# Time mix of a hybrid decoder step: the k and r projections as seven Strassen block products instead of eight

## The chip, the cores and the metric

One core of one Trainium2 chip runs the whole step. The metric is the device time of one execution in microseconds (us). TensorE does the matrix products, VectorE (DVE in the rows), ScalarE (ACT) and GpSimd (POOL) the elementwise work, and SyncE (SP) only starts transfers. All arithmetic is fp32.

## What is computed

The step has two branches fed by one input projection: latent attention (A) and an RWKV-7 time mix (B). This case is about B. Its input is `h` of 576 tokens (512 of a prompt and 8 samples of 8), 1024 channels; its projections r, k and v are 1024 x 1024 each:

```python
cols = jnp.einsum('btd,dn->btn', h, w_in)
...
xs = p + (prev - p) * mu_shift          # prev: the token before
r, wl, k, v, al = xs[..., :o1], xs[..., o1:o2], xs[..., o2:o3], xs[..., o3:o4], xs[..., o4:]
...
S = S * d_t - Sk[..., None] * (kk_t * a_t) + v_t[..., None] * k_t
```

A recurrence over the tokens follows (computed in chunks of 128 tokens, with the inverse of a triangular matrix per chunk and head), then a group norm, gates and the output projections.

## The kernel before

`rwkv` holds the time mix. Its main loop has eight passes, `i` = 0 to 7, one for each pair of heads (128 channels). Pass `i` does the recurrence of pair `i` and, between its dependent steps, the projections of pair `p = i + 1` (passes 0 to 6; the last pass fills the same places with gate projections, `gate_parts`). Each engine has its own queue, written out by hand in order, and waits on semaphores.

- The inverse has levels 0 to 5. At each, TensorE does `level_w`, ScalarE copies the result (`level` of the scalar part), TensorE does `level_x`, VectorE takes that up (`level` of the vector part: `copy_predicated` and a transpose), and the next level begins. TensorE fills the time between `level_w` and `level_x` with pieces of `project(p, q, steps)`: `q` = 0 is k, 1 is r, 2 is v. One step is one product of a 128 x 128 weight block with 288 tokens, and a projection is 16 steps: two halves of the tokens (`F0`, `F1`, 288 each) times eight blocks of channels. The profile counts two instructions for each fp32 step.
- A half's eight steps add up in one bank of PSUM. ScalarE then copies it to `px` and, scaled, to `xs` (`projected`); VectorE adds the token before it (`mix`). `keys`, `key_norms`, `key_max`, `roots` and `key_normed` normalise k. `decays` are three exponentials.
- At the start of a pass TensorE does the Gram matrices. VectorE takes the banks with `copy_predicated` (L2506, L2509) and starts the inverse with `begin_inverse`: four (or two) `copy_predicated` of 32 partitions (L2516) per group of units, whose mask `lev` and data `gram` are both in SBUF. TensorE's `token_major` (L1819) waits until VectorE has emptied the banks.
- GpSimd does little in this loop: `first_columns`, `last_columns` and `powers` (L1546, a power of 10 columns). Its queue is in that order: `powers(i - 1)` ends shortly after pass `i` began.
- `w` has four slots of weights; SP loads the next pair's into a slot (`next_w`) when the last product that reads it is done.

The stage behind the loop (`merge`) computes its own projections already by seven block products: `stationary_sums` and `moving_sums` there form operand sums on GpSimd (L2850 to L2866), `keep` copies partial sums on ScalarE, and `add` adds on VectorE (L3043 from PSUM and SBUF, L3045 from two SBUF tensors).

Of the kernel before, what the change touches and what calls it, by code (L numbers as in the profile page):

```python
# [13 lines left out]
P = 128  # L14
# [608 lines left out]
def prompt(nc, I, M):  # L623

    with ExitStack() as ctx:
# [32 lines left out]
        def _(sp):  # L658
# [769 lines left out]
EARLY_IN = 16 * (2 + 17 + 2)  # L1428
# [19 lines left out]
def rwkv(nc, I, O, M):  # L1448

    with ExitStack() as ctx:  # L1450
        sb = lambda name, shape: ctx.enter_context(nc.sbuf_tensor("rw_" + name, shape, F32))
        NU, C5, LAST = 2 * NB, NB, NP - 1
        gram, tm = sb("gram", [P, NU, 4, P]), sb("tm", [P, C5, 3, P])
# [7 lines left out]
        XT0, W5, Phi = sb("XT0", [RH, 2 * PB, RH]), sb("W5", [P, 2 * PB, RH]), sb("Phi", [P, PB, RH])  # L1461
        s_in, bkT, S = sb("s_in", [RH, BD, P]), sb("bkT", [P, 2, P]), sb("S", [P, PB + 1, P])
        bonus, M.ob = sb("bonus", [P, 2, USED]), sb("ob", [P, USED])
        o, om = sb("o", [P, NU, RH]), sb("om", [P, 2, NU])
        s_out, M.uvm = sb("s_out", [RH, BD, P]), sb("uvm", [P, BD, P])
        snT, oc, uv, sp_out, cen, gx, g = M.snT, M.oc, M.uv, M.sp_out, M.cen, M.gx, M.g
# [15 lines left out]
        lora_mm, sa_sb, proj, px_sb, pxs0, mixed, shc_sb = (sem(n) for n in ("lora_mm", "sa_sb", "proj", "px_sb", "pxs0", "mixed", "shc_sb"))  # L1482
        cum, expd, kkd, kf1_sb, kk_sum, kk_max, rooted, rk_prod, rk_sum, bonus_in, bonus_sb, prepared = (
# [14 lines left out]
        halves = (slice(0, RH), slice(RH, P))  # L1498
        F0, F1 = slice(0, HT), slice(HT, USED)
        ORDER, GATE_SLOT = (1, 0, 2), (1, 0, 2, 1)  # L1500
# [20 lines left out]
        def _(pool):  # L1521
# [25 lines left out]

            pool.wait_ge(tail.pv, G * (BD - 1))
# [32 lines left out]
        def _(sp):  # L1581
# [17 lines left out]
            def store_branch(p):  # L1599
                sp.wait_ge(ob_sb, p + 1)  # L1600
                sp.dma_start(M.ob_dram[:, p, 0:USED], M.ob[:, :]).then_inc(ob_stored, 16)
# [20 lines left out]
            def next_w(p, q):  # L1622
                sp.wait_ge(proj, 6 * p + 2 * q + 2)
# [38 lines left out]
            sp.wait_ge(M.cleared, 2)  # L1662
            store_branch(LAST - 1)
# [22 lines left out]
        def _(pe):  # L1686
# [43 lines left out]
            def project(p, q, steps):  # L1730
                for t in steps:
# [3 lines left out]
                    if k == 0:  # L1735
                        if q == 0:
                            if p:
                                pe.wait_ge(sa_sb, 4 * p + 3 + h)
                        elif q == 1:
                            pe.wait_ge(px_sb, 6 * p + h + 1)  # L1740
                        else:
                            pe.wait_ge(kk_max, p + 1)
                    last = mm(bank[h][:, 0:HT], w[:, ORDER[q], k, :], M.hT[:, k, (F0, F1)[h]], start=(k == 0), stop=(k == KT - 1))  # L1743
                    if k == KT - 1:
                        last.then_inc(proj, 1)

# [153 lines left out]
            def old_states(i):  # L1900
# [4 lines left out]
                for b in range(BD):  # L1905
                    last = tr(bank[2][:, b * RH:(b + 1) * RH], s_in[:, b, :], M.ident[0:RH, 0:RH])
# [79 lines left out]
            def out_to_tokens(i):  # L1986
                pe.wait_ge(oc_sb, i + 1)
                for c in range(PB):
                    last = tr(bank[6][:, c * P:(c + 1) * P], oc[:, c * P:(c + 1) * P], M.ident[:, :])
# [48 lines left out]
            for i in range(NP):  # L2038
# [39 lines left out]
                if more:  # L2078
                    project(p, 0, range(0, 5))
# [3 lines left out]
                if more:  # L2083
                    project(p, 0, range(5, 11))
# [5 lines left out]
                if more:  # L2090
                    project(p, 0, range(11, 16))
# [5 lines left out]
                if more:  # L2097
                    project(p, 1, range(0, 4))
# [5 lines left out]
                if more:  # L2104
                    project(p, 1, range(4, 8))
# [3 lines left out]
                if more:  # L2109
                    project(p, 1, range(8, 12))  # L2110
# [5 lines left out]
                if more:  # L2116
                    project(p, 1, range(12, 16))
# [5 lines left out]
                level_x(i, 5)  # L2123
                if more:
# [3 lines left out]
                prompt_y(i)  # L2128
# [40 lines left out]
        def _(act):  # L2169
# [21 lines left out]
            def projected(p, q, h):  # L2191
                n = ORDER[q]
                keep = M.omm[:, 8 * n + p:8 * n + p + 1]
                act.wait_ge(proj, 6 * p + 2 * q + h + 1)
# [1040 lines left out]
```

## Time and profile before

| | |
|---|---|
| median of 3 runs | 1559.08 us (1559.01 to 1562.05) |
| profiled execution, device time | 1559.9 us |
| its span, first to last instruction | 1558.3 us |
| mean granted TensorE clock | 0.992 of full speed |
| TensorE busy | 1509.3 us, 97% |
| VectorE, ScalarE, GpSimd busy | 823.8, 543.6, 223.6 us |
| main loop of the time mix | 686 to 1287 us, a pass of about 75 us |

The span is the time between the first and the last instruction; the device time is 1.6 us longer. Busy time of TensorE counts modelled ends of overlapping instructions, so starts of consecutive blocks are the better measure of what a block costs.

### The profile page before, as it was taken

Reading aid. Unit: us, or ns where it says so; the run is one execution under the profiler, and the core shown is the slowest. Engines: PE = TensorE matmul, PEld = TensorE weight load, DVE = VectorE, ACT = ScalarE, POOL = GpSimd, SP = SyncE. Lnnn points to the kernel's source line nnn. Section 1 sums busy time; section 2 is a strip of 40 time slices with the busy share of each in tenths; the row PEclk is TensorE's granted clock in tenths of the full one; section 3 lists DMA queues with packets and bytes.
Section 4 is the critical chain, followed back from the end, with each engine's and each line's share of the span. In section 5 each row is a group of like instructions: output and inputs, shape, how many; then the busy total and the mean of one; then the engine's idle time right before and its main releaser. Section 6 shows DMA issues by size and latency. Waiting matters only on the chain.

```text
span 1558.3 us, 36214 instructions
## 1 busy us (share of the span) xinstructions
PE 1509.3 (97%) x14666; PEld 1102.8 (71%) x14666; DVE 823.8 (53%) x1653; ACT 543.6 (35%) x1327; POOL 223.6 (14%) x279
## 2 busy tenths in 40 slices
PE   6999999999999999989999999999999999999998
PEld 4455576777888888767676767677777777777753
DVE  3154455557777777464656566656656522023422
ACT  3056445441222222336353535353535222210000
POOL 0000141220112120110000000000000045355200
PEclk9999999989999999999999999999999999999999
DMA  9713688832566663411111111111111116342302
GB/s 328 288 54 108 182 227 281 221 96 72 138 161 164 159 161 101 115 42 38 30 51 31 50 32 50 32 50 40 41 51 34 46 35 193 92 147 75 115 14 74
DMA packets 190674, 164.35 MB, mean 105 GB/s; under 512 B 38458, under 2 KB 169530, under 8 KB 189484
## 3 DMA queue, kind: packets, MB, share of 16 engines
q1 hardware_dynamic: 181228, 126.47, 29.0%
q0 software_dynamic: 8352, 32.52, 6.9%
q10 hardware_dynamic: 928, 3.05, 0.6%
q8 instruction: 116, 1.90, 0.5%
q14 instruction: 50, 0.41, 0.1%
HBM read 136.44 MB, written 25.56 MB: 104 GB/s over the span
## 4 chain that ended last, share of the span: by engine, by line
PE 83%; DVE 6%; ACT 5%; DVEq 2%; DMA 2%; issue 1%; SPq 0%; POOL 0%; ACTq 0%
PE me_bank L2929 12%; PE rw_bank L1743 10%; PE sa_psOs L1197 7%; PE sa_psS L1152 7%; PE me_bank L2949 4%; PE pr_psZ L738 3%; PE fr_bankL L307 2%; PE rw_bank L1782 2%; PE fr_bankL L247 2%; PE pr_psS L726 2%; PE sa_psT L1162 2%; DVE rw_gram L2506 2%; PE rw_bank L1844 2%; PE pr_psO L757 1%; PE rw_bank L1863 1%
## 5 line engine op out<-in xcount | busy, mean ns | idle before, releaser
L1743 PE MATMUL rw_bank<-hT,big 128*128 128x288 f32 x672 | 182.8, 417 | 0.0
L1743 PEld LDWEIGHTS rw_bank<-hT,big 128*128 128x128 f32 x672 | 121.9, 189 | 32.1 <-issue 1.2
L1254 ACT COPY kpe<-sa_psS 128x512 f32<-128x512 f32 x64 | 34.4, 589 | 137.3 <-PE sa_psS L1152 137.3
L738 PE MATMUL pr_psZ<-hT,qlT 128*128 128x288 f32 x256 | 74.1, 410 | 0.6 <-DVE pr_zraw L838 0.6
L1768 PE MATMUL rw_bank<-hT,big 128*128 128x288 f32 x256 | 73.5, 421 | 0.0
L1541 POOL COPY shc<-prep 128x3 f32<-128x3 f32 x8 | 1.5, 188 | 471.1 <-ACT rw_xs L2208 471.1
L2988 ACT COPY big<-me_bank 128x288 f32<-128x288 f32 x42 | 16.7, 398 | 144.8 <-PE me_bank L2929 144.8
L738 PEld LDWEIGHTS pr_psZ<-hT,qlT 128*128 128x128 f32 x256 | 47.5, 192 | 21.7 <-issue 10.1
L2526 DVE COPY_PREDICATED rw_X<-lev,rw_bank 128x128 f32<-128x128 int32 (+1 forms) x80 | 20.9, 261 | 77.5 <-PE rw_bank L1863 77.5
L1197 PE MATMUL sa_psOs<-big,sa_ST 128*128 128x257 f32 x256 | 60.3, 386 | 0.0
L1197 PE MATMUL sa_psOs<-pages,sa_ST 128*128 128x257 f32 x256 | 60.3, 385 | 0.0
L997 POOL DMA_DIRECT2D big<-in_cache_kv x68 | 37.6, 552 | 156.1 <-issue 156.1
L1768 PEld LDWEIGHTS rw_bank<-hT,big 128*128 128x128 f32 x256 | 44.9, 189 | 20.1 <-issue 11.5
L1343 DVE TENSOR_TENSOR sa_ST<-sa_psT,kinvp 128x512 f32<-128x512 f32 x64 | 42.9, 679 | 28.7 <-PE sa_psT L1162 28.6
L1197 PEld LDWEIGHTS sa_psOs<-pages,sa_ST 128*128 128x128 f32 x256 | 47.1, 189 | 11.0 <-issue 4.4
L1197 PEld LDWEIGHTS sa_psOs<-big,sa_ST 128*128 128x128 f32 x256 | 47.0, 190 | 11.3 <-issue 5.0
L997 POOL DMA_DIRECT2D pages<-in_cache_kv x68 | 37.5, 552 | 117.8 <-issue 117.2
L2929 PE MATMUL me_bank<-prep,me_arena 128*128 128x288 f32 x208 | 53.4, 406 | 0.0
L882 ACT COPY pr_pT<-pr_psT 128x128 f32<-128x128 f32 (+3 forms) x64 | 27.2, 425 | 59.9 <-PE pr_psT L747 59.9
L2929 PEld LDWEIGHTS me_bank<-prep,me_arena 128*128 128x128 f32 x208 | 39.5, 190 | 10.9
L1264 ACT ACTIVATE sa_ST<-sa_ST 128x1024 f32<-128x1024 f32 x32 | 33.8, 1057 | 37.5 <-DVE sa_ST L1366 36.8
L726 PE MATMUL pr_psS<-pr_kh,pr_qh 96*128 96x128 f32 (+3 forms) x128 | 45.8, 440 | 0.1
(564 smaller groups left out, 3373.2 us busy)
## 6 DMA issues: line engine op xcount, KB each, us to landing
big<-in_w_in SPq DMA_DIRECT2D x44, 512.0 KB, 4.0
big<-in_cache_kv POOLq DMA_DIRECT2D x68, 128.0 KB, 3.7
pages<-in_cache_kv POOLq DMA_DIRECT2D x68, 128.0 KB, 3.2
fr_wada<-in_w_ada SPq DMA_DIRECT2D x8, 1024.0 KB, 11.7
big<-in_cache_kv SPq DMA_DIRECT2D x60, 128.0 KB, 2.9
pages<-in_cache_kv SPq DMA_DIRECT2D x60, 128.0 KB, 3.1
qk_scratch<-oaT SPq DMA_DIRECT2D x32, 192.0 KB, 2.6
fr_wada<-in_w_ada SPq DMA_DIRECT2D x2, 2048.0 KB, 11.0
```

The costliest lines, as they stand in the source:

```text
L726: nc.tensor.matmul(psS[u % 3][:, 0:cols(u)], qh[hp % 2][:, hh, qb * P:(qb + 1) * P], kh[hp % 2][:, hh, 0:cols(u)], start=True, stop=True). ...
L738: last = nc.tensor.matmul(psZ[h][:, 0:HT], M.wz[hp % 2][:, k, :], M.hT[:, k, h * HT:(h + 1) * HT], start=(k == 0), stop=(k == KT - 1))
L997: e.dma_start(M.pages[s % 2][q * QP:(q + 1) * QP, g, :, 0:KL], src).then_inc(landed, 16)
L1152: done = nc.tensor.matmul(psS[:, b, 0:2 * P], q4[n % 2][rows, a, :], cT(i)[rows, a, :], start=False, stop=(a == NCB - 1))
L1197: done = nc.tensor.matmul(psO[:, 0:C1], STs[s % 2][:, GP * g + c, :], M.pages[s % 2][:, g, c, :], start=(g == 0 and c == 0), stop=False)
L1254: nc.scalar.copy(S.rearrange("q (c p j) -> q p c j", c=2 * GP, p=GP)[:, :, cs, :], got[:, :, cs, :]).then_inc(copied, 1)
L1264: nc.scalar.activation(part, part, ACT.Exp, scale=SCALE).then_inc(exped, 1)
L1343: v.tensor_tensor(group, psT[g % 2][:, :].rearrange("p (a h t) -> p a h t", h=H, t=TD), bc(ki, TD, 3), ALU.mult).then_inc(weighted, 1)
L1743: last = mm(bank[h][:, 0:HT], w[:, ORDER[q], k, :], M.hT[:, k, (F0, F1)[h]], start=(k == 0), stop=(k == KT - 1))
L1768: last = mm(bank[h][:, 0:HT], w[:, 3, k, :], M.hT[:, k, (F0, F1)[h]], start=(k == 0), stop=(k == KT - 1))
L2929: last = nc.tensor.matmul(into[:, 0:HT], st[:, k, :], mv[:, k, :], start=(k == 0 and n in (1, 2, 7)), stop=(k == KT // 2 - 1), skip_group_ ...
L2949: last = nc.tensor.matmul(out_bank[o][:, :], mT[k][:, b * P:(b + 1) * P], wo[k][:, n * 512:(n + 1) * 512], start=(k == 0), stop=(k == KT - 1))
```

## The change

k and r of pair `p` become one product of a 2 x 2 block matrix (k and r by low and high half of the 1024 channels) with a 2 x 2 block matrix (low and high channels by `F0` and `F1`). Strassen's form in Winograd's variant needs seven block products of four steps each, 28 steps in place of 32, for each of the seven pairs of the loop. The products are run in the order 1, 2, 6, 5, 3, 7, 4 into two banks. v stays as it was, and so do the projections of pair 0.

- GpSimd forms the sums of the moving operand once, in pass 0 (`moving_sums`: 16 operations of 288 columns), and those of the weights for each pair (`stationary_sums`: 4 of 128 columns, one of 512, and, after products 1 and 2 are done, 4 of 128 and one of 512 that overwrite weights in place).
- ScalarE copies the running sum of bank 0 to `px` after products 1, 6 and 5 (`keep_partial`), and scales from SBUF (`scaled_from_sbuf`).
- VectorE adds bank 1 to what was kept (`add_partial`), three times a pair.
- `key_norms` moves behind `prompt_y` on TensorE, `keys` behind `level(i, 5)` on ScalarE, `mix(p, 0)` behind `level(i, 4)` on VectorE.
- Room for the sums comes from sharing: `gate` is saved to DRAM early and loaded back in the last pass, `ob` shares with `bonus`, `oc` with `RT`, `XT0` with `W5`, `snT` with the spare columns of `hT`.

```diff
+            sp.wait_ge(M.front_done, 1)
+            sp.dma_start(M.gate_dram, M.gate[:, :]).then_inc(M.early_in, 16)
...
+            def moving_sums():
+                pool.wait_ge(prepared, 1)
+                pool.wait_ge(M.early_in, EARLY_IN)
+                for k in range(K4):
+                    q.tensor_tensor(T3[k], M.hT[:, K4 + k, F1], M.hT[:, k, F1], ALU.subtract)
+                pool.drain()
+                pool.wait_ge(M.oa_stored, 32)
+                for k in range(K4):
+                    q.tensor_tensor(T2[k], T3[k], M.hT[:, k, F0], ALU.add)
+                pool.drain()
+                for k in range(K4):
+                    q.tensor_tensor(T4[k], M.hT[:, K4 + k, F0], T2[k], ALU.subtract)
+                for k in range(K4):
+                    last = q.tensor_tensor(T1[k], M.hT[:, k, F1], M.hT[:, k, F0], ALU.subtract)
+                last.then_inc(summed, 1)
+
+            def stationary_sums(p):
+                a1, a2 = w[:, 1, :, :], w[:, 0, :, :]
+                pool.wait_ge(w_in[1], 16 * p + 16)
+                pool.wait_ge(w_in[0], 16 * p + 16)
+                for k in range(K4):
+                    q.tensor_tensor(S1[k], a2[:, k, :], a2[:, K4 + k, :], ALU.add)
+                pool.drain()
+                q.tensor_tensor(a2[:, 0:K4, :], a1[:, 0:K4, :], a2[:, 0:K4, :], ALU.subtract)
+                pool.drain()
+                pool.wait_ge(proj, proj_of(p, 1))
+                for k in range(K4):
+                    last = q.tensor_tensor(a1[:, k, :], S1[k], a1[:, k, :], ALU.subtract)
+                last.then_inc(summed, 1)
+                pool.drain()
+                pool.wait_ge(proj, proj_of(p, 2))
+                q.tensor_tensor(a1[:, K4:KT, :], a1[:, K4:KT, :], a1[:, 0:K4, :], ALU.subtract).then_inc(summed, 1)
...
             for i in range(NP):
+                if i == 0:
+                    moving_sums()
                 if i < LAST:
                     first_columns(i + 1)
+                    stationary_sums(i + 1)
                     last_columns(i + 1)
...
+            sp.dma_start(M.gate[:, :], M.gate_dram).then_inc(M.fixed_in, 16)
...
+            def multiply(p, n):
+                a1, a2 = w[:, 1, :, :], w[:, 0, :, :]
+                low, high = slice(0, K4), slice(K4, KT)
+                if n == 1:
+                    pe.wait_ge(w_in[1], 16 * p + 16)
+                    pe.wait_ge(sa_sb, 4 * p + 3)
+                elif n == 2:
+                    pe.wait_ge(sa_sb, 4 * p + 4)
+                elif n == 6:
+                    pe.wait_ge(kept, kept_of(p, 1))
+                    pe.wait_ge(summed, summed_of(p, 2))
+                elif n == 5:
+                    pe.wait_ge(kept, kept_of(p, 6))
+                elif n == 3:
+                    pe.wait_ge(kept, kept_of(p, 5))
+                    pe.wait_ge(summed, summed_of(p, 4))
+                elif n == 7:
+                    pe.wait_ge(added, added_of(p, 11))
+                elif n == 4:
+                    pe.wait_ge(w_in[0], 16 * p + 16)
+                    pe.wait_ge(added, added_of(p, 22))
...
                 level_w(i, 1)
                 if more:
-                    project(p, 0, range(0, 5))
+                    multiply(p, 1)
...
                 level_x(i, 1)
                 if more:
-                    project(p, 0, range(5, 11))
+                    multiply(p, 2)
...
                 level_w(i, 2)
                 if more:
-                    project(p, 0, range(11, 16))
+                    multiply(p, 6)
...
                 level_w(i, 3)
                 if more:
-                    project(p, 1, range(0, 4))
+                    multiply(p, 5)
...
                 level_x(i, 3)
                 if more:
-                    project(p, 1, range(4, 8))
+                    multiply(p, 3)
...
                 level_w(i, 4)
                 if more:
-                    project(p, 1, range(8, 12))
+                    multiply(p, 7)
...
                 level_x(i, 4)
                 if more:
-                    project(p, 1, range(12, 16))
+                    multiply(p, 4)
...
                 level_x(i, 5)
+                prompt_y(i)
                 if more:
                     key_norms(p)
                 else:
                     gate_parts(range(46, 47))
-                prompt_y(i)
...
                 level(i, 3)
-                if not more:
+                if more:
+                    keep_partial(p, 5)
+                    scaled_from_sbuf(p, 1, 0)
+                else:
                     gate_sigmoid(2)
                 blocks_in_place(i, 2)
                 if more:
                     decays(p)
+                    second_keys(p)
...
                 level(i, 4)
                 if more:
-                    projected(p, 1, 0)
+                    scaled_from_sbuf(p, 0, 1)
...
+                level(i, 5)
                 if more:
                     keys(p)
-                level(i, 5)
-                if more:
-                    projected(p, 1, 1)
+                    scaled_from_sbuf(p, 0, 0)
```

## Rows read from the trace of the kernel before

**Rows 1.** The page, part 1.

```profile
PE 1509.3 (97%) x14666; PEld 1102.8 (71%) x14666; DVE 823.8 (53%) x1653; ACT 543.6 (35%) x1327; POOL 223.6 (14%) x279
```

**Rows 2.** Windows: us, busy PE, PEld, DVE, ACT, POOL, then PEclk.

```profile
835.00:910.00 75.00, 72.87 (x1076) 54.61 (x1076) 45.76 (x102) 34.48 (x90) 2.47 (x4) 1.00 0.16 42
```

**Rows 3.** Waits of TensorE, 700 to 1260: total, times, longest.

```profile
PE rw_bank L1819 <- DVE rw_gram L2509: 5.3, 7, 1.1
PE rw_bank L1953 <- ACT rw_Y L2283: 2.0, 7, 0.3
```

**Rows 4.** Timeline of TensorE, 922 to 992: start, duration, line.

```profile
928.21 2.69 PE L1743 MATMUL rw_bank<-hT,big 128*128 128x288 f32 x10
930.83 0.88 PE L1863 MATMUL rw_bank<-rw_X,rw_W 32*32 32x32 f32 x72
931.64 3.18 PE L1743 MATMUL rw_bank<-hT,big 128*128 128x288 f32 x12
934.65 0.71 PE L1883 MATMUL rw_bank<-ident_sb,rw_o 128*128 128x128 f32 x5
...
942.26 2.21 PE L1743 MATMUL rw_bank<-hT,big 128*128 128x288 f32 x8
944.40 1.08 PE L1891 MATMUL rw_bank<-rw_uvm,rw_bkT 128*64 128x512 f32 x4
...
957.17 1.14 PE L1870 MATMUL rw_bank<-rw_XF,rw_W 64*64 64x64 f32 x16
```

**Rows 5.** Timeline of ScalarE, 922 to 992.

```profile
943.15 1.28 ACT L2186 ACT_TABLE_LOAD   x1
...
946.18 0.20 ACT L2189 ACTIVATE g<-gx 128x12 f32<-128x12 f32 x1
948.71 0.26 ACT L2244 COPY rw_W<-rw_bank 32x128 f32<-32x128 f32 x1 [2.34 <-PE rw_bank L1847]
...
954.20 1.06 ACT L2267 COPY rw_s_out<-rw_bank 64x512 f32<-64x512 f32 x2
...
956.75 0.64 ACT L2247 COPY rw_W<-rw_bank 64x256 f32<-64x256 f32 x2
957.41 0.35 ACT L2206 COPY prep<-rw_bank 128x224 f32<-128x224 f32 x1
...
958.15 1.17 ACT L2273 COPY rw_s0p<-rw_bank 64x512 f32<-64x512 f32 x2
```

**Rows 6.** Timeline of all engines, 763.9 to 765.5.

```profile
763.93 0.22 POOL L1537 COPY prep<-ssT 128x24 f32<-128x24 f32 x1
...
764.42 1.22 DVE L2516 COPY_PREDICATED rw_X<-lev,rw_gram 32x128 f32<-32x128 int32 x4
```

**Rows 7.** Lines by form, GpSimd, 880 to 1560.

```profile
L2861 POOL TENSOR_TENSOR me_arena<-big 128x512 f32<-128x512 f32 x10 | 12.9, 1292 | 50.6 <-DMA big<-in_w_pb 20.9 <-DMA big<-in_w_pa 16.1 <-DMA big<-in_w_in 13.6
...
L2850 POOL TENSOR_TENSOR prep<-hT 128x1152 f32<-128x1152 f32 x1 | 2.6, 2627 | 48.4 <-ACT rw_Y L2278 48.4
```

**Rows 8.** Line L3043 on VectorE: ns min, median, max.

```profile
L3043 DVE TENSOR_TENSOR big<-me_bank,big x24: 457/458/458, 1382.7 to 1496.5; 128x288 f32<-128x288 f32 x24
```

**Rows 9.** Line L3045 on VectorE, the same columns.

```profile
L3045 DVE TENSOR_TENSOR prep<-prep,big x8: 458/1110/2703, 1383.3 to 1455.0; 128x288 f32<-128x288 f32 x8
```

**Rows 10.** Timeline of all engines, 1400.1 to 1403.3.

```profile
1400.47 2.64 POOL L2851 TENSOR_TENSOR prep<-me_arena 128x1152 f32<-128x1152 f32 x1
1400.72 2.70 DVE L3045 TENSOR_TENSOR prep<-prep,big 128x288 f32<-128x288 f32 x1
```

**Rows 11.** Line L2516 on VectorE, columns as in rows 8.

```profile
L2516 DVE COPY_PREDICATED rw_X<-lev,rw_gram x80: 219/294/307, 691.6 to 1224.1; 32x128 f32<-32x128 int32 x64, 32x64 f32<-32x64 int32 x16
```

**Rows 12.** Timeline of VectorE, 691 to 699.

```profile
691.63 1.22 DVE L2516 COPY_PREDICATED rw_X<-lev,rw_gram 32x128 f32<-32x128 int32 x4
...
695.76 1.22 DVE L2516 COPY_PREDICATED rw_X<-lev,rw_gram 32x128 f32<-32x128 int32 x4
```

**Rows 13.** Windows of pass 0, columns as in rows 2.

```profile
691.00:694.00 3.00, 0.53 (x7) 0.16 (x3) 2.79 (x8) 0.00 (x0) 0.00 (x0) 1.00 0.01 1
694.00:697.40 3.40, 3.40 (x19) 2.74 (x20) 3.19 (x9) 0.98 (x4) 0.00 (x0) 0.52 0.00 0
```

More of the change, by code:

```diff
@@ L1425 @@
 HT = USED // 2
-EARLY_IN = 16 * (2 + 17 + 2)
+EARLY_IN = 16 * (1 + 2 + 17 + 2)
 def _load_vectors(sp, I, M):
@@ L1745, in project @@
                         last.then_inc(proj, 1)
+            def multiply(p, n):
[19 more added lines that the diff above has]
+                    pe.wait_ge(added, added_of(p, 22))
+                into = bank[1 if n in (2, 7, 4) else 0][:, 0:HT]
+                st = {1: a1[:, low, :], 2: a1[:, high, :], 3: a1[:, high, :], 4: a2[:, high, :], 6: a1[:, low, :], 7: a2[:, low, :]}
+                for k in range(K4):
+                    held = S1[k] if n == 5 else st[n][:, k, :]
+                    moving = {1: M.hT[:, k, F0], 2: M.hT[:, K4 + k, F0], 3: M.hT[:, K4 + k, F1], 4: T4[k], 5: T1[k], 6: T2[k], 7: T3[k]}[n]
+                    last = mm(into, held, moving, start=(k == 0 and n in (1, 2, 7)), stop=(k == K4 - 1), skip_group_check=True)
+                last.then_inc(proj, 1)
             def first_projections(q, h):
@@ L1905, in old_states @@
                 for b in range(BD):
-                    last = tr(bank[2][:, b * RH:(b + 1) * RH], s_in[:, b, :], M.ident[0:RH, 0:RH])
+                    last = tr(bank[2][:, b * RH:(b + 1) * RH], s_in[:, b, :], M.ident[halves[1], halves[1]])
                 last.then_inc(s_tr, 1)
@@ L1988, in out_to_tokens @@
                 for c in range(PB):
-                    last = tr(bank[6][:, c * P:(c + 1) * P], oc[:, c * P:(c + 1) * P], M.ident[:, :])
+                    last = tr(bank[6][:, c * P:(c + 1) * P], oc_of(i)[:, c * P:(c + 1) * P], M.ident[:, :])
                 last.then_inc(oc_tr, 1)
@@ L2301, in out_channels @@
                     act.wait_ge(M.oa_stored, 32)
-                a.copy(oc[:, :], bank[6][:, :]).then_inc(oc_sb, 1)
+                a.copy(oc_of(i), bank[6][:, :]).then_inc(oc_sb, 1)
             def last_state(i):
@@ L2465, in mix, with add_partial @@
                 stt(by_b(xs[:, n, SEQ:USED]), pxs[:, n, :, 0:TD], mu, by_b(xs[:, n, SEQ:USED]), ALU.mult, ALU.add).then_inc(mixed, 1)
+            def add_partial(p, n):
+                dve.wait_ge(proj, proj_of(p, {11: 2, 22: 7, 21: 4}[n]))
+                dve.wait_ge(kept, kept_of(p, {11: 1, 22: 5, 21: 6}[n]))
+                got = bank[1][:, 0:HT]
+                if n == 22:
+                    mine, own = px[:, 0, HT + 1:SEQ + 1], pxs[:, 0, :, 1:TD + 1]
+                    tt(mine, got[:, 0:SEQ - HT], mine, ALU.add)
+                    tt(own, by_b(got[:, SEQ - HT:HT]), own, ALU.add).then_inc(added, 1)
+                else:
+                    mine = px[:, 1 if n == 11 else 0, 1:HT + 1]
+                    tt(mine, got, mine, ALU.add).then_inc(added, 1)
             def key_scaled(p):
@@ L2687, in _ @@
                 if more:
+                    add_partial(p, 11)
                     cumulated(p)
@@ L2692, in _ @@
                 if more:
+                    add_partial(p, 22)
+                level(i, 4)
+                if more:
                     mix(p, 0)
                     dr()
-                level(i, 4)
-                if more:
+                    add_partial(p, 21)
                     key_scaled(p)
```

93 lines of the change are left out of this document (68 added, 25 removed).

## The prediction

> **What bounds the kernel now.** I read the page first: TensorE is busy 97% of the span [rows 1]. That is the whole step, so I asked for windows of the main loop. A pass takes 75 us and TensorE works 72.87 of them, VectorE 45.76, ScalarE 34.48, GpSimd 2.47, at the full granted clock [rows 2]. The reader should see two things: products taken out of this loop shorten it unless something is late, and GpSimd has room by its busy time. Then the waits of TensorE: over seven passes 5.3 us at L1819 for VectorE's emptying of the Gram banks and 2.0 us at L1953 for ScalarE [rows 3]. These are small, but they name the two places where another engine, not TensorE, sets the end: the start of a pass (VectorE) and the end of the inverse (ScalarE). A delay of VectorE in the first place goes through in full. Last I read the timelines of one steady pass, engine by engine.
>
> **What the change removes.** The blocks it shortens are those after `level_w(1)`, `level_x(1)` and `level_w(2)`: 5, 6 and 5 steps become 4 each. By starts of what follows, a block of ten instructions (five steps) takes 930.83 - 928.21 = 2.62 us, of twelve 934.65 - 931.64 = 3.01, and of eight 944.40 - 942.26 = 2.14 [rows 4]. The third block has ten, like the first. So a pass loses 2.62 + 3.01 + 2.62 - 3 x 2.14 = 1.83 us, and seven passes 12.8 us. The other four blocks had four steps and keep them.
>
> **Whether the shorter blocks still cover the inverse.** `level_x(1)` needs ScalarE's copies, which end some 1.1 us before it now; it comes 0.5 us earlier. `level_w(2)` needs VectorE, which ends more than 2 us before it; it comes 1.4 us earlier. I take nothing for both.
>
> **Waits of the new products.** The copies, adds and sums work on small pieces and each stands one or two TensorE blocks ahead of its reader. Product 6 waits for four GpSimd sums of 128 columns. One of 512 takes 1.29 us and one of 1152 takes 2.63 [rows 7], so 2.1 ns a column and 0.2 us fixed: 0.46 us for 128, 1.9 us for four. They start when product 1 ends, and product 6 comes after `level_x(1)`, product 2, the transposes of the output and `level_w(2)`, together 4.2 us: hidden, with 2 us to spare. The sum that product 3 needs (1.3 us) has some 9 us. `add_partial` of product 7 is 0.7 us long, under 0.97 + 0.6 us of TensorE work before product 4. All hidden; without its cover each would cost its own length once a pass.
>
> **ScalarE.** Its work is about the same, but in another order. I count from the end of `level_w(3)`, 942.26. Before, the table load for the exponentials began at 943.15 and the last of them was issued at 946.18, 3.0 us later, and then ScalarE waited 2.34 us for `level_w(4)` [rows 5]. Now it first waits for product 5 (2.14 us), keeps it (0.35), scales k (0.39) and does `blocks_in_place` (0.5): the load begins at 3.5 after 942.26 instead of 0.9, the exponentials end at 6.7, `second_keys` (three operations, 0.74 by 957.41 to 958.15) at 7.5, and the four copies of `level(4)` of 0.27 at 8.6. TensorE asks for them at 9.6. So 1 us of slack is left of what was over 2. In pass 0 the two sample products of the previous pair are missing from TensorE (2.0 us), so there TensorE asks at 7.6 and waits: I take 0.75 us, once. Then comes the stretch up to `level(5)`. Before, its copies began at 956.75 and TensorE's `level_x(5)` at 957.17 [rows 4, 5], so ScalarE was just in time. After: VectorE's add ends at 9.3, then 0.5 + 3.7 + 1.1 us of scaling, `blocks_in_place` and state copies, so the first copy is ready at 14.9 plus the semaphore, against 14.8 before. `keys` has been moved behind it, which pays for the later start. I take 0.1 us a pass, 0.6. Up to `transitions` my two sums come to the same 19.85 us, so the moved `key_norms` costs nothing: its 1.05 us cover moves from before `prompt_y` to before the wait for ScalarE's `Y`. VectorE's `key_max` comes 1.7 us later, but VectorE had 1.6 us idle before the first state, and TensorE's projection of v comes after 1.2 us of `transitions`. Together: **+1.35 us**.
>
> **GpSimd against VectorE.** This is the term that decides. In the stage behind the loop, which already does this, the add of a bank and one SBUF tensor takes 457 to 458 ns in all 24 cases [rows 8], also while GpSimd works. The product of two SBUF tensors of the same size takes from 458 up to 2703 ns [rows 9]. The longest one was issued at 1400.72 during a GpSimd subtraction (1400.47, 2.64 us long) and ended at 1403.42, just 0.31 us after that one's end at 1403.11 [rows 10]. So it did not run slower: it waited until 0.15 us before GpSimd's instruction ended and then ran its 0.46. The Trainium skill says the same (SBUF — State Buffer, section "Who interferes with whom": a VectorE instruction with two SBUF inputs and a GpSimd instruction that reads SBUF exclude each other for their whole length); the trace agrees.
>
> Where do the new GpSimd instructions meet such an instruction? In passes 1 to 6 the weights have long landed, so the first sums begin right after `first_columns` (763.93 + 0.22), and VectorE's four L2516 of `begin_inverse` run at 764.42 to 765.64 [rows 6]. Mask and data of these are both in SBUF. Four sums of 0.46 us lie beside four copies of 0.305 us. Of a sum, about 0.3 us excludes the other engine (0.46 less 0.15), and GpSimd takes its turn between any two copies. Three to four waits of 0.2 to 0.3 give 0.8 us a pass. The row of 512 columns then meets only the L2506, whose data are in PSUM. Now a copy never takes more than 307 ns [rows 11], and no row shows L2516 under GpSimd's sums. Bounds: 0 from below (a predicated copy might not be excluded), and from above 4 x 0.46 = 1.84, each copy waiting for a whole sum; a gain is excluded. I take 0.8, since L2516 is like L3045 in its inputs. It passes to TensorE, which waits for VectorE in this place [rows 3]. Six passes: **+4.8 us** (0 to 11.0).
>
> Pass 0 is worse: sixteen moving sums of 0.19 + 288 x 0.0021 = 0.80 us run from about 685.5 on. By my count twelve are still to come after 689, when the samples' output has been stored, and last to 699 or later. The L2516 lie at 691.63 and 695.76, four each, and two more near 698 [rows 12]. Each excluded stretch is 0.65 us. The first four wait some 2.2 us, of the second four two wait for moving sums and two for weight sums (1.6), and the last two wait near 0.9 beside the sum of 512. That is 4.7 us of VectorE, from which I take the slack of `level_w(0)` and the transposes, about 1.2: **+3.5 us** (0 to 6.5, ten whole waits). Something comes with it: TensorE idles 2.5 us there now and is then granted 0.52 of full speed, the lower of its two levels (1.2 against 2.4 GHz), for 3.4 us [rows 13]. A longer idle can bring that again, for up to 1 us more; it stays in the upper bound.
>
> **Transfers.** The save of `gate` (512 KB) stands on SP's queue behind the last store of the front stage, ahead of a load with time to spare; the load back in the last pass stands ahead of the branch store, of which nothing waits soon. The weights of k and r are reloaded up to 10 us later than now, still some 25 us before their reader. The store from `bonus` has 30 us. Nothing.
>
> **The sum.** -12.8 + 1.35 + 4.8 + 3.5 = -3.15 us, against the profiled execution's 1559.9 us: 1556.75. The median of the runs shown is 0.8 us lower, so there 1559.08 - 3.15 = 1555.9.
>
> **Rivals.**
> *The copies are not excluded.* If L2516 passes GpSimd freely, only -12.8 + 1.35 = -11.45 remains: 1547.6. For it: no row shows it stretched. Against it: its two inputs lie as those of L3045. Chance 0.2.
> *VectorE waits in full (the other side).* If each L2516 waits for a whole sum, passes 1 to 6 cost 11.0, pass 0 6.5 and the clock 1: -12.8 + 1.35 + 18.5 = +7.1, 1566; from 1.5 us a pass on the change is slower. The place is the start of every pass, the mechanism VectorE's turn against GpSimd's. Against it: in rows 10 the wait ended before GpSimd's record did. Chance 0.15, most of it below 1563.
> *ScalarE becomes the bound of the inverse.* If its order costs 0.5 us a pass beyond what I found at `level(4)` or `level(5)`, 3.5 us come on top and the time is 1559.4, no change. For it: 1 us of slack where there were 2, and none at `level(5)`. Chance 0.2.
> My forecast, 1553 to 1558.5 by itself, has 0.45.
>
> **Numbers.** Within 0.2%, 3.1 us, is what a measurement can't tell from no change. My forecast lies on that border. Half of its chance and all of the first rival's is faster, with a little of the others: faster 0.48; within 0.2%: 0.37; slower 0.15. The range takes in the first rival and most of the second: 1547 to 1562.5.
>
> **What would show it.** Of the 288-column instructions on `w` in the loop 56 are gone (7 x 4 steps x 2). TensorE's wait at L1819 for VectorE grows by about 0.8 us a pass. L2516 has a longest value of 0.5 us or more instead of 0.307 [rows 11], and in pass 0 near 0.9; if it stays near 0.3 the first rival is true. TensorE's waits for ScalarE at `level_x(4)` appear in pass 0 alone; if in each pass, the third rival. The prediction is wrong if a pass from 760 on is shortened by much other than 0.9 us, or if TensorE waits at one of the new products.

## The result and the profile after

The changed kernel takes 1581.93 us (median of 4 runs, 1577.1 to 1587.97), the kernel before 1560.57 beside it (4 runs, 1559.01 to 1563.73). The ratio is 1.0138, 95% interval 1.0121 to 1.0155: slower by 1.4%, on the other side of no change from the forecast and outside the range. The profiled execution took 1587.97 us; its span is 28.0 us longer than before (1586.3 against 1558.3). It is the slowest of the four: the medians differ by 21.4 us only. Traces below are of profiled executions, and gains between kernels are differences of medians.

The page of the changed kernel, part 1, against [rows 1]:

```profile
PE 1521.1 (96%) x14610; PEld 1112.6 (70%) x14610; DVE 847.7 (53%) x1681; ACT 546.5 (34%) x1334; POOL 277.6 (17%) x365
```

TensorE has 56 instructions fewer, as counted, and is busy 11.8 us longer: what is left runs slower. The windows of the changed kernel show where. The first one answers to [rows 2], the second is the loop as a whole, and the others lie around single stalls:

```profile
835.00:910.00 75.00, 71.17 (x1005) 52.89 (x1000) 45.63 (x102) 34.88 (x91) 8.44 (x14) 0.91 0.17 42
760.00:1240.00 480.00, 457.15 (x6447) 341.63 (x6443) 297.23 (x646) 210.95 (x550) 51.02 (x86) 0.95 0.16 41
...
808.00:813.00 5.00, 3.77 (x57) 2.81 (x47) 3.77 (x10) 4.81 (x16) 0.00 (x0) 1.00 0.01 4
813.00:819.60 6.60, 6.60 (x40) 6.14 (x41) 0.83 (x2) 4.43 (x9) 0.00 (x0) 0.50 0.76 161
...
859.00:868.00 9.00, 8.97 (x235) 6.22 (x236) 3.93 (x12) 4.46 (x15) 0.00 (x0) 0.62 0.04 11
868.00:895.00 27.00, 25.77 (x525) 19.62 (x524) 15.44 (x40) 14.98 (x44) 2.96 (x5) 1.00 0.11 32
895.00:904.00 9.00, 9.00 (x72) 7.92 (x71) 2.33 (x6) 6.00 (x10) 0.00 (x0) 0.62 0.55 118
```

The last three numbers of a row are the granted clock, the DMA share and GB/s. Before, the clock of 760 to 1240 was 1.00; now it is 0.95. TensorE falls to half speed (0.50, the 1.2 GHz level) behind some of its stalls and is back at 1.00 some microseconds later. The waits of TensorE say what the stalls are, 700 to 1260, against [rows 3]:

```profile
PE rw_bank L1901 <- DVE rw_gram L2637: 12.3, 8, 1.8
PE rw_bank L1931 <- ACT rw_XF L2367: 6.0, 7, 1.2
PE rw_bank L1901 <- DVE rw_gram L2634: 3.0, 6, 0.8
PE rw_bank L1988 <- ACT rw_states L2380: 2.6, 6, 0.4
```

L1901 is `token_major` (L1819 before), L1931 `level_w(5)`, L1988 `old_states`. There are two places per pass, as the prediction's first part named them: its start, behind VectorE, and the end of the inverse, behind ScalarE. No row names one of the new products. In pass 0 `level_x(4)` waits 0.3 us for ScalarE (0.75 forecast).

**The start of a pass.** The timeline of GpSimd in pass 1, 769.9 to 773.4:

```profile
769.97 0.22 POOL L1554 COPY prep<-ssT 128x24 f32<-128x24 f32 x1
770.13 0.44 POOL L1586 TENSOR_TENSOR gate<-big 128x128 f32<-128x128 f32 x1
770.55 0.44 POOL L1586 TENSOR_TENSOR free_tail<-big 128x128 f32<-128x128 f32 x1
770.96 0.50 POOL L1586 TENSOR_TENSOR rw_free_c<-big 128x128 f32<-128x128 f32 x1
771.42 0.50 POOL L1586 TENSOR_TENSOR rw_free_a<-big 128x128 f32<-128x128 f32 x1
772.06 1.26 POOL L1588 TENSOR_TENSOR big<-big 128x512 f32<-128x512 f32 x1
```

The four copies of `begin_inverse` beside them, in VectorE's timeline:

```profile
770.49 2.99 DVE L2644 COPY_PREDICATED rw_X<-lev,rw_gram 32x128 f32<-32x128 int32 x4
```

The same four in the view of their source line (shortest, median, longest in ns; first and last start):

```profile
L2644 DVE COPY_PREDICATED rw_X<-lev,rw_gram x4: 449/556/1389, 770.5 to 772.1; 32x128 f32<-32x128 int32 x4
```

The group takes 2.99 us where it took 1.22 [rows 6]. Three of the copies take 0.45 to 0.66 us and the fourth 1.389. The fourth starts with the row of 512 columns (772.1 and 772.06) and ends at 773.48 (770.49 + 2.99), some 0.15 us behind it (772.06 + 1.26 = 773.32). So the reader should look at the longest value, not at the mean: a mean of 0.75 would suggest that each copy waited for one short sum. Passes 2 to 6 look the same, groups of 2.93 to 2.96 us with a longest copy of 1393 to 1404 ns. GpSimd pays little: 0.44 to 0.52 us a sum, where 0.46 was estimated from [rows 7] and e1 has 0.45 to 0.46 with no copy beside; the third and fourth sum are each 0.05 longer.

**The end of the inverse.** The timeline of TensorE in pass 1, 809 to 814 (in brackets the idle time before and what ended it):

```profile
809.33 1.13 PE L1826 MATMUL rw_bank<-big 128*128 128x288 f32 x4
810.39 0.68 PE L1931 MATMUL rw_bank<-rw_W,rw_gram 64*64 64x64 f32 x8
811.86 0.65 PE L1931 MATMUL rw_bank<-rw_W,rw_gram 64*64 64x64 f32 x8 [0.79 <-ACT rw_XF L2367]
812.95 1.00 PE L1988 MATMUL rw_bank<-ident_sb,rw_states 64*128 64x64 f32 x8 [0.44 <-ACT rw_states L2380]
```

ScalarE's timeline ahead of it:

```profile
807.42 0.48 ACT L2298 ACTIVATE rw_xs<-prep,omm 128x224 f32<-128x224 f32 x1 [0.80 <-DVE prep L2590]
807.81 0.33 ACT L2299 ACTIVATE rw_xs<-prep,omm 128x64 f32<-128x64 f32 x1
808.05 0.59 ACT L2365 COPY rw_W<-rw_XT 32x128 f32<-32x128 f32 x2
808.65 1.21 ACT L2367 COPY rw_XF<-rw_X 32x128 f32<-32x128 f32 x4
809.88 0.60 ACT L2365 COPY rw_W<-rw_XT 32x128 f32<-32x128 f32 x2
810.50 1.21 ACT L2367 COPY rw_XF<-rw_X 32x128 f32<-32x128 f32 x4
```

The second half of `level_w(5)` waits for the last L2367 of `blocks_in_place`, which ends at 811.71. Ahead of `blocks_in_place` stand the idle 0.80 us and the 0.63 us of `scaled_from_sbuf(p, 0, 1)`. At 813 the clock falls to 0.50, and `prompt_y` (16 instructions) takes 3.45 us where it took 1.95.

**Which stalls the slow clock follows.** The two kinds of stall differ. TensorE's wait at the start of a pass is 1.84 us in pass 1 and in pass 2:

```profile
779.14 0.33 PE L1901 MATMUL rw_bank<-ident_sb,rw_ZR 128*128 128x128 f32 x1 [1.84 <-DVE rw_gram L2637]
...
859.03 0.33 PE L1901 MATMUL rw_bank<-ident_sb,rw_ZR 128*128 128x128 f32 x1 [1.84 <-DVE rw_gram L2637]
```

Behind the second the clock is 0.62 for 9 us (above); behind the first it stays at 1.00, and so it does at the start of passes 3 to 6. The end of the inverse has a stretch of 7 to 8 us at about half speed in every one of passes 0 to 6. In pass 3, behind its start and behind its inverse:

```profile
943.00:946.00 3.00, 2.87 (x139) 2.18 (x126) 2.44 (x8) 2.13 (x5) 0.00 (x0) 1.00 0.04 9
...
976.00:979.00 3.00, 3.00 (x15) 3.00 (x16) 0.33 (x1) 1.04 (x3) 0.00 (x0) 0.50 0.88 225
```

### The profile page after: what moved, and what is told of

It reads as the page before. It is cut to its first block, busy times and chain, and to the rows that moved or that the text cites. A ratio compares the mean times of both kernels' runs of the same rounds, so it can differ in the third digit from the quotient of the medians.

```text
span 1586.3 us, 36264 instructions
## 1 busy us (share of the span) xinstructions
PE 1521.1 (96%) x14610; PEld 1112.6 (70%) x14610; DVE 847.7 (53%) x1681; ACT 546.5 (34%) x1334; POOL 277.6 (17%) x365
## 4 chain that ended last, share of the span: by engine, by line
PE 83%; DVE 8%; ACT 4%; DVEq 3%; issue 1%; DMA 1%; SPq 0%; POOL 0%; ACTq 0%
PE me_bank L3058 12%; PE sa_psOs L1199 7%; PE sa_psS L1154 7%; PE rw_bank L1826 5%; PE rw_bank L1796 4%; PE me_bank L3078 3%; PE pr_psZ L740 3%; PE fr_bankL L307 2%; PE rw_bank L1864 2%; PE pr_psS L728 2%; PE fr_bankL L247 2%; DVE rw_gram L2634 2%; PE sa_psT L1164 2%; PE rw_bank L2025 2%; DVE rw_X L2644 2%; PE rw_bank L1926 2%
## 5 line engine op out<-in xcount | busy, mean ns | idle before, releaser
L1850 PE MATMUL rw_bank<-hT,big 128*128 128x288 f32 x256 | 73.5, 421 | 0.0
L999 POOL DMA_DIRECT2D big<-in_cache_kv x68 | 37.6, 553 | 156.5 <-issue 156.5
L1796 PE MATMUL rw_bank<-hT,big 128*128 128x288 f32 x224 | 61.1, 416 | 0.0
L1850 PEld LDWEIGHTS rw_bank<-hT,big 128*128 128x128 f32 x256 | 44.9, 189 | 20.1 <-issue 11.5
L1796 PEld LDWEIGHTS rw_bank<-hT,big 128*128 128x128 f32 x224 | 40.8, 189 | 11.7 <-issue 1.2
L1826 PE MATMUL rw_bank<-hT,big 128*128 128x288 f32 x168 | 47.0, 424 | 0.0
## 6 DMA issues: line engine op xcount, KB each, us to landing
fr_wada<-in_w_ada SPq DMA_DIRECT2D x8, 1024.0 KB, 11.8
```

The lines of the kernel that those rows point to most:

```text
L999: e.dma_start(M.pages[s % 2][q * QP:(q + 1) * QP, g, :, 0:KL], src).then_inc(landed, 16)
L1826: last = mm(into, held, moving, start=(k == 0 and n in (1, 2, 7)), stop=(k == K4 - 1), skip_group_check=True)
L1850: last = mm(bank[h][:, 0:HT], w[:, 3, k, :], M.hT[:, k, (F0, F1)[h]], start=(k == 0), stop=(k == KT - 1))
```

## The experiments

"After" is the changed kernel. The first column of times is the median of the experiment's runs; the ratio is that of the mean times, to the kernel before, run beside it. Its medians there lie from 1560.05 to 1562.14, so a difference of a microsecond or two between two experiments is not shown. The other columns are from the profiled execution. "Copies" is the group of four copies at the start of passes 1 to 6, "ScalarE waits" is TensorE's wait for ScalarE in `level_w(5)` and `old_states` of all passes, and the clock is that of 760 to 1240.

| kernel | us (lowest to highest, runs) | ratio, 95% interval | copies, us | ScalarE waits, us | clock |
|---|---|---|---|---|---|
| before | 1560.57 (4) | 1 | 1.22 | 0 | 1.00 |
| after | 1581.93 (4) | 1.0138 (1.0121 to 1.0155) | 2.93 to 2.99 | 8.6 | 0.95 |
| e1, sums after the copies | 1567.64 (1564.91 to 1572.53, 9) | 1.0055 (1.0037 to 1.0072) | 1.22 to 1.24 | 8.6 | 0.98 |
| e2, scaling later | 1559.71 (1555.23 to 1567.04, 10) | 0.9995 (0.9977 to 1.0014) | up to 2.96 | 0.6 | 0.98 |
| e3, both | 1544.3 (1540.43 to 1546.33, 4) | 0.9894 (0.9863 to 0.9925) | 1.2 | 0.6 | 1.00 |
| e4, unused products in the stalls | 1561.27 (1558.47 to 1565.8, 10) | 1.0012 (0.9998 to 1.0025) | 1.69, then 2.96 | 0.3 | 1.00 |
| e5, sums beside the Gram copies | 1551.3 (1548.11 to 1557.83, 8) | 0.994 (0.9925 to 0.9956) | 1.22, next group 1.7 | 0.6 | 1.00 |
| e6, before with shared buffers | 1560.95 (1554.86 to 1563.59, 10) | 0.9996 (0.9982 to 1.0009) | 1.22 | 0 | 1.00 |
| e7, e6 with the sums | 1573.87 (1573.44 to 1576.45, 4) | 1.0091 (1.0072 to 1.011) | 1.68, 2.63, then 2.93 to 2.96 | 0 | 0.99 |
| e8, e3 with pass 0 mended | 1543.08 (1542.23 to 1545.29, 4) | 0.9884 (0.9866 to 0.9902) | 1.2 | 0.6 | 1.00 |
| e9, e3 once more | 1545.63 (1544.26 to 1546.12, 4) | 0.9896 (0.988 to 0.9913) | 1.2 | 0.6 | 1.00 |
| e10, long sum later | 1573.6 (1565.42 to 1574.44, 6) | 1.0074 (1.0052 to 1.0095) | 1.68 to 1.86 | 8.6 | 0.97 |
| e11, long sum in four | 1575.09 (1570.1 to 1581.03, 6) | 1.01 (1.0075 to 1.0124) | 1.69, then 2.13 to 2.15 | 8.6 | 0.97 |

**e1: sums after the copies.**

```diff
+                pool.wait_ge(x_sb[2], inv_g(2, p - 1) + 1)   # head of stationary_sums
```

> The changed kernel, but GpSimd's sums of the weights start only when begin_inverse of the pass is over, so that none lies beside the predicated copies with two SBUF inputs. Theory A (the copies wait for GpSimd, which costs 1.77 us a pass directly, and TensorE's longer idle there brings a slower clock in some passes): those copies fall back to 1.22 us for four in passes 1 to 6 (from 2.99), TensorE's idle before token_major falls to what it was before the change, and the time falls by 10 to 20 us, to 1562 to 1572. Theory B (the loss comes from ScalarE's order before level_w(5)): only the 1.77 us a pass come back, 10.6 us at most, and the clock stays near 0.976. Theory C (it is the moving sums of pass 0 or the new products): no change beyond 3 us.

14.3 us came back. The copies give 6 x 1.74 = 10.4 of them; the rest, 3.9, came with the clock, 0.98 instead of 0.95.

**e2: scaling behind `keys`.**

```diff
                 level(i, 4)
-                if more:
-                    scaled_from_sbuf(p, 0, 1)
                 blocks_in_place(i, 0)
...
                     keys(p)
+                    scaled_from_sbuf(p, 0, 1)
                     scaled_from_sbuf(p, 0, 0)
```

> The changed kernel, but ScalarE scales the second half of r after level(5) instead of ahead of blocks_in_place, so that nothing in front of blocks_in_place waits for VectorE's add. Theory B: TensorE's waits at level_w(5) (6.0 us over seven passes) and at old_states (2.6 us) nearly vanish, and with them the slow clock that follows in those passes: the time falls by 10 to 20 us, to 1562 to 1572. Theory A: only the waits of 1.2 us a pass come back, 8 us at most, and the granted clock stays low after the start of the passes.

22.2 us came back, more than expected: 8.0 us are the waits, and 2.6 are copies, since in passes 1 and 2 the group takes 1.69 us here. The rest, some 11.6 us or half, was the clock. It still falls in e2, behind the starts of passes 2 to 5, where the changed kernel shows it behind that of pass 2 alone.

**e3 and e9: both edits.**

> Both edits together. If stalls and the clock that they bring are the whole cause, what remains is the saving of 1.83 us a pass, less the cost of the moving sums in pass 0 (4 to 6 us): granted clock back at 0.99, 1549 to 1556, faster than before the change. If something else in the new order costs time, it stays above 1560.

> e3_both once more, as the measure for e8_pass0 on the same chip: 1544.3 within 1.5 us.

37.6 us came back, more than expected, and the kernel is faster than before by 1.06%. Of them 10.4 + 8.0 = 18.4 us are copies and waits, which leaves 19.2 for the clock. The waits of TensorE in e3, 700 to 1260, have one wait for VectorE as in [rows 3], none for `Y`, and this one for ScalarE, in pass 0 (beside the 0.3 us of `level_x(4)` there):

```profile
PE rw_bank L1902 <- DVE rw_gram L2637: 5.7, 8, 1.0
...
PE rw_bank L1932 <- ACT rw_XF L2368: 0.6, 1, 0.6
```

**e4: work in the stalls, waits left as they are.** The rival of "the waits cost their own length" was that their main price is the clock. Here TensorE does seven products of 224 columns a pass of which nothing is used, at the three places where it waits:

```diff
+                    if i and c == PB - 1:          # before the last token_major but one
+                        pe.wait_ge(gram_sb, NU * i + 8)
+                        filler(4, 3)
...
+                    if lv == 5 and gr == 1 and i < LAST:   # in level_w(5)
+                        pe.wait_ge(px_sb, 6 * (i + 1) + 2)
+                        filler(2, 0)
...
+                if i < LAST:                        # before old_states
+                    filler(1, 0)
```

> The changed kernel with extra matrix products that compute nothing used, put where TensorE waits: four before the last token_major but one of passes 1 to 7 (about 1.5 us), two inside level_w(5) and one before old_states (about 1.1 us together). TensorE has 2.6 us more work a pass and no wait is taken away. If the slow clock is brought by these waits, the granted clock goes from 0.975 to 0.99 and the time falls by 10 to 20 us, to 1562 to 1572, with more work on the engine. If the slow clock has nothing to do with the waits, the time rises by 0 to 10 us and the clock stays.

With more work, and the copies as slow as in the changed kernel in five of six passes, the time falls by 20.7 us (some 1.2 of them are the copies of pass 1), and the clock is 1.00. The window of the loop in e4:

```profile
760.00:1240.00 480.00, 472.98 (x6902) 351.58 (x6900) 310.59 (x682) 216.98 (x569) 52.71 (x85) 1.00 0.17 42
```

The copies' source line in pass 2 of e4:

```profile
L2656 DVE COPY_PREDICATED rw_X<-lev,rw_gram x4: 447/536/1395, 840.2 to 841.8; 32x128 f32<-32x128 int32 x4
```

This shows that TensorE's idleness, not the new products, brings the clock down, and sizes the clock's part at about 19 us of a median execution. It fills both kinds of stall at once and doesn't tell them apart.

**e5: sums beside the copies from PSUM.** e2, with the sums started when the first `begin_inverse` is done:

```diff
+                pool.wait_ge(x_sb[0], inv_g(0, p - 1) + 1)   # head of stationary_sums
```

> As e2_scale_later, but GpSimd's sums start when the first begin_inverse of the pass is over, so that the four sums of 128 columns lie beside the copies out of the Gram banks (mask in SBUF, data in PSUM), and the end of the sum of 512 beside the second begin_inverse. If only VectorE instructions with two SBUF inputs wait for GpSimd: the copies out of the banks keep 2.55 us for four, the first begin_inverse has 1.22 us, the second takes up to 1 us more than 1.22, and the time lies between e3_both and e2_scale_later, 1545 to 1555. If any VectorE instruction that reads SBUF waits: the copies out of the banks take 4 us for four and the time is that of e2_scale_later or above.

GpSimd's sums run from 770.28 to 773.40 here. The view of VectorE's two source lines:

```profile
L2634 DVE COPY_PREDICATED rw_gram<-see,rw_bank x4: 702/723/747, 770.1 to 771.9; 128x512 f32<-128x512 int32 x4
...
L2644 DVE COPY_PREDICATED rw_X<-lev,rw_gram x4: 297/303/776, 772.8 to 774.2; 32x128 f32<-32x128 int32 x4
```

Copies whose data are in PSUM pass almost freely: these four take 2.56 us beside the sums and 2.52 without, in e1. Of the L2644 from 772.8 on the longest takes 0.776: it meets the end of the row of 512. So the prediction was right on which instructions collide. The Trainium skill (SBUF — State Buffer, section "Who interferes with whom") says that a VectorE instruction with at most one input in SBUF, outside the 2-port modes, does not contend with GpSimd, and that one with two does when GpSimd reads SBUF; these rows agree.

**e6 and e7: the transfers and sharing alone, then the sums alone.** e7 lets GpSimd make the four sums and the long one at the start of passes 1 to 6 into spare room, and nothing reads them (SP waits for them before it reloads weights); k and r are projected as before.

```diff
                     first_columns(i + 1)
+                    if i:
+                        sums_beside(i + 1)
```

> The kernel before with nothing but the shared buffers of the change (gate saved to DRAM and loaded back, ob in bonus, oc in RT, XT0 in W5, snT in the spare columns of hT); eight products and the old order of all engines. Expected within 1.5 us of the kernel before, 1560. If the sharing had a part in the loss, it shows here as more than 3 us.

> As e6_share_only, and in passes 1 to 6 GpSimd also forms the four sums of 128 columns and the one of 512 at the start of the pass, into spare room; nothing reads them, and the eight products stay. This is the cost of GpSimd beside begin_inverse by itself. Theory A: the four predicated copies take 3.0 us instead of 1.22, each pass is 1.8 us longer, 10.6 us together, plus the clock where TensorE's idle grows: 1570 to 1576. If the wait were hidden in the old order: 1560.

Sharing buffers, saving `gate` and loading it back cost nothing. The sums alone cost 12.9 us over e6, of which the six groups of copies are 8.8. e7 also shows what makes the size. The view of the copies' source line (L2581 here) around the start of pass 1 and of pass 2, with copies of later groups among them:

```profile
L2581 DVE COPY_PREDICATED rw_X<-lev,rw_gram x10: 221/300/451, 765.8 to 773.8; 32x128 f32<-32x128 int32 x8, 32x64 f32<-32x64 int32 x2
L2581 DVE COPY_PREDICATED rw_X<-lev,rw_gram x7: 220/297/1403, 843.7 to 851.4; 32x128 f32<-32x128 int32 x5, 32x64 f32<-32x64 int32 x2
```

Where no copy takes longer than 0.451 us the group takes 1.68 us, and from pass 2 on, where one takes 1.4, 2.63 to 2.96. That raised the question for the last two runs: does each copy pay a share, or the fourth alone the most?

**e10 and e11: the long sum moved, or cut in four.** Each is the changed kernel with one edit.

```diff
                 pool.drain()
+                pool.wait_ge(x_sb[0], inv_g(0, p - 1) + 1)      # e10
-                q.tensor_tensor(a2[:, 0:K4, :], a1[:, 0:K4, :], a2[:, 0:K4, :], ALU.subtract)
+                for k in range(K4):                             # e11
+                    q.tensor_tensor(a2[:, k, :], a1[:, k, :], a2[:, k, :], ALU.subtract)
```

> The changed kernel, in which GpSimd's one sum of 512 columns at the start of a pass waits until VectorE has done the first four copies of begin_inverse and their transpose; the four sums of 128 columns stay beside the copies. Theory A (the fourth copy pays): in the changed kernel single copies of passes 1 to 6 take 0.45 to 0.66 us three times and 1.39 to 1.40 us once, and the long one starts with the row of 512 (772.06) and ends 0.1 us behind it. Then three copies keep their 0.65 us together, the fourth falls back to 0.3, the group of four takes 1.9 us, and no copy is longer than 0.7 us in passes 1 to 6. Directly 6 x 1.1 = 6.6 us, and more if TensorE's clock falls less often: 1565 to 1576 us. Theory B (each copy waits for one whole short sum, whatever follows): the group stays at 2.9 to 3.0 us and the time at 1582 within 2 us.

> The changed kernel, in which GpSimd's one sum of 512 columns at the start of a pass is made as four of 128 columns (each 0.46 us, 1.7 us together instead of 1.26); nothing else moves. Theory A (a copy waits for the rest of whichever sum it meets, so the length of one sum sets the price): the fourth copy meets a sum of 0.46 instead of 1.26 us, so it takes about 0.45 us instead of 1.40, the group of four 2.0 us, and the longest copy of passes 1 to 6 is under 0.7 us: directly 6 x 0.95 = 5.7 us, 1566 to 1577 us. Theory B (GpSimd's total work beside the copies sets the price): the group stays at 2.9 us or grows, 1582 us or more.

The copies of passes 1 to 6, first e10, then e11:

```profile
L2645 DVE COPY_PREDICATED rw_X<-lev,rw_gram x70: 220/297/616, 769.3 to 1236.2; 32x128 f32<-32x128 int32 x56, 32x64 f32<-32x64 int32 x14
```

```profile
L2645 DVE COPY_PREDICATED rw_X<-lev,rw_gram x70: 220/298/624, 768.1 to 1236.6; 32x128 f32<-32x128 int32 x56, 32x64 f32<-32x64 int32 x14
```

Theory A holds in both. With the long sum away, the group takes 1.68 to 1.86 us: three copies lose 0.46 to 0.64 together. With the same work cut in four it takes 2.13 to 2.15 from pass 2 on, though GpSimd works longer beside the copies (1.75 us for the four pieces, 1.26 in one). A copy pays for the rest of the instruction that it meets, so the length of one sum sets the price. 8.3 and 6.8 us came back, for 6 x 1.22 = 7.3 and 5.3 us of copies.

**e8: pass 0 mended too.** On e3: the moving sums that only products 5 and 4 need stand behind the sums in place, and the first ones that follow T3 start after `begin_inverse`.

```diff
                 pool.wait_ge(M.oa_stored, 32)
+                pool.wait_ge(x_sb[2], 1)
...
+                if p == 1:
+                    later_moving_sums(1)
...
+                if p == 1:
+                    later_moving_sums(4)
```

> As e3_both, and in pass 0 the moving sums but the first four start only after the third begin_inverse, in the order in which the products need them (the sums of product 6, then 5, then 4). The eight predicated copies of pass 0 fall from 6.0 to 2.5 us, TensorE's longest wait from 4.5 to 2.5 us, and the slow clock after it gets shorter: 3 to 6 us faster than e3_both, 1538 to 1542. If TensorE then waits for the later sums instead, no gain.

Pass 0 of the changed kernel, VectorE's timeline of the copies (1.22, 1.22 and 0.46 us before, [rows 12] has the first two):

```profile
691.64 3.27 DVE L2644 COPY_PREDICATED rw_X<-lev,rw_gram 32x128 f32<-32x128 int32 x4
...
697.87 2.71 DVE L2644 COPY_PREDICATED rw_X<-lev,rw_gram 32x128 f32<-32x128 int32 x4
...
701.71 0.62 DVE L2644 COPY_PREDICATED rw_X<-lev,rw_gram 32x64 f32<-32x64 int32 x2
```

TensorE's wait behind the first of them, 2.47 us before:

```profile
696.07 0.45 PE L1901 MATMUL rw_bank<-ident_sb,rw_ZR 128*128 128x128 f32 x1 [4.55 <-DVE rw_gram L2634]
```

The same copies in e8:

```profile
690.65 1.22 DVE L2653 COPY_PREDICATED rw_X<-lev,rw_gram 32x128 f32<-32x128 int32 x4
...
694.81 1.23 DVE L2653 COPY_PREDICATED rw_X<-lev,rw_gram 32x128 f32<-32x128 int32 x4
...
697.17 0.46 DVE L2653 COPY_PREDICATED rw_X<-lev,rw_gram 32x64 f32<-32x64 int32 x2
```

The span falls by 2.7 us against e3 (1544.7 to 1542.0) and by 2.2 against e9; the medians of e9 and e8, run beside each other, differ by 2.55 us, and their runs overlap. That is less than the 3 to 6 us expected: the copies are back at their old times, but TensorE is still at half speed from about 699 to 706, as long as from 693 to 701 in e3. e8 is the fastest kernel here, 1.16% under the one before.

## Why the prediction was wrong

The account of the span, changed kernel against the one before:

| term | forecast | found | where from |
|---|---|---|---|
| 56 instructions fewer | -12.8 | -12.8 | count of the page; a block of eight still starts 2.14 us ahead of the next |
| moved `key_norms` | 0 | -3.4 | 7 x 0.5, below |
| copies, passes 1 to 6 | +4.8 | +10.4 | 6 x 1.74 |
| moving sums of pass 0 | +3.5 | +2.7 | e8 against e3 |
| ScalarE | +1.35 | +8.6 | waits of TensorE: 6.0 + 2.6 |
| clock | 0 | +22.5 | the rest up to 28.0 |
| sum | -3.15 | +28.0 | |

The 28.0 us are those of the slowest of four executions. On the medians, 21.4 us, the same terms leave 15.9 for the clock; e3 gives 19.2 for it and e4 about 19. So the clock cost 16 to 22 us.

In e8 all but the first two terms should be gone: 1558.3 - 12.8 - 3.4 = 1542.1, against a span of 1542.0. That it fits to 0.1 us is luck in part. By the starts of the first copies of each pass, passes 1 to 6 take 436.5 us in e8 and 452.2 before, 15.7 less, where 6 x (1.83 + 0.5) = 14.0 were counted. Pass 0 takes 73.3 us in e8 and 72.8 before: it is no shorter, 2.9 us over its account, and its slow clock, 7 us where it lasted 3.4 [rows 13], is some 1.8 of them.

**The step that failed most: the clock.** "A longer idle can bring that again, for up to 1 us more; it stays in the upper bound" was said of pass 0 alone. I had read that the clock was 1.00 in a steady pass [rows 2] and half behind the 2.5 us of pass 0 [rows 13], but I priced a new stall of every pass at its own length. In the changed kernel the 0.79 and 0.44 us close together brought 7 to 8 us at half speed in each of passes 1 to 6 (in pass 0 one wait of 1.2 us did), and the 1.8 us at the start of a pass did in pass 2 alone. So a term that makes TensorE wait can be too small by a factor: e2 removed 8.0 us of waits and 2.6 of copies and gained 22.2. The gains add: e1 and e2 gave back 14.3 + 22.2 = 36.5 and e3 37.6. Of e1's gain 3.9 us are clock, of e2's about 11.6.

The other two terms are smaller. With the copies at 10.4 the prediction's sum is +2.45 us, 1562.4, just inside its range. All measured terms but the clock come to +5.5, 1565.4, against 1587.97 in that execution.

**The second: GpSimd against VectorE, 0.8 where 1.74 was measured.** The mechanism was right, and so were the place and the three short waits: e10 leaves 0.46 to 0.64 a pass. What failed is "the row of 512 columns then meets only the L2506". It contradicts my own numbers: sums of 0.46 us from 764.15 on end at 765.99, and copies that start at 764.42 and take 1.22 + 0.8 end at 766.44, so the last one runs beside the row of 512. The second rival came out at nearly this size, 11.0 us, but by another mechanism: not each copy pays a whole short sum, the fourth pays the long one. e10 and e11 tell these apart. (The prediction's "from 1.5 us a pass on the change is slower" doesn't follow from its own terms: -12.8 + 1.35 + 3.5 = -7.95 is used up at 1.33 us a pass.)

**The third: ScalarE.** The times were right to a tenth. From the end of `level_w(3)` I counted 8.6 us to the end of `level(4)`'s copies; it is 806.63 - 798.03 = 8.6. I then asked who waits for ScalarE's next copies of `level(5)`, and never who waits for `blocks_in_place`: `level_w(5)` itself reads what it writes, and `old_states` the state copies. Both come before `level(5)`. The third rival, ScalarE as the bound of the inverse at 0.5 us a pass, was the true one in kind; it was 1.2 a pass, and the clock on top.

**Right:** the saving; that no new product waits; that shared buffers and transfers cost nothing (e6); which instructions collide (e5). The moving sums of pass 0 came near their size: its copies took 6.6 us where they took 2.9, 3.7 more (4.7 forecast), of which e8 gave back 2.2 to 2.7 us of time (3.5 forecast).

**Better than forecast: `key_norms`.** I gave it nothing, since its cover only moves. In e3 the wait of 0.3 us for `Y` is gone, and from the first instruction of `new_states` to the projection of v it is 958.48 - 957.02 = 1.46 us where it was 963.29 - 961.34 = 1.95. All seven passes show it, 1.44 to 1.46 us in e3 and 1.94 to 1.95 before, so I count 0.5 us seven times; that the move causes it is read from the two timelines and was not tried alone.

Left open: why the same wait of 1.84 us brings the slow clock in one pass and not in another, and so what a stall of that length costs. In e10 and e11 the clock is 0.97 and the gain over the direct one 1.0 and 1.5 us, in e1 it is 0.98 and 3.9 us; the runs of one kernel differ by some us.

## What to carry to other kernels

Where the matrix engine is busy 97% of the time, a new stall of a microsecond in a repeated stage can cost several times its length: look in the trace for what the granted clock did behind the stalls that are already there, and carry that into every pass. When a step is moved on an engine, list all readers of everything queued behind it, not only the next one. Put helper work on GpSimd beside VectorE instructions that read PSUM, and where it must lie beside ones with two inputs in SBUF, make it short instructions.

## What the runs showed of the hardware

- VectorE's copies with mask and data in SBUF and GpSimd's sums take turns. Each copy that met a sum ended some 0.15 us behind that sum's end (773.48 against 773.32 for the long one; 771.6 against 771.46 for one of 0.50), whether the sum was 0.5 or 1.26 us long. The same kind of copy with data in PSUM was hardly touched (2.56 against 2.52 us for four). GpSimd lost about 0.05 us on two of four sums.
- Two short stalls of TensorE (0.79 and 0.44 us, within 2 us) were followed by 6.6 us at a granted clock of 0.50, in the same way in passes 1 to 6. One of 1.84 us was followed by a window of 9 us at 0.62 in pass 2 and by 1.00 in passes 1 and 3 to 6. Products that nothing reads, put into the stalls, kept the clock at 1.00 in passes 1 to 6 and made the kernel 20.7 us faster.
